# Expert results added back by slot matmuls in SBUF instead of by a trip through DRAM

## The reference

```
x    = layer_norm(ALPHA * x + merged @ w_o)                       # x1, 264 x 2048
combine[t, e]: router; top-1 of 4 expert groups, in it top-2 experts, weights sum to 1
for e in range(16):
    h = silu(xt @ w_gate[e]) * (xt @ w_up[e])                     # 2048 -> 1024
    y = y + combine[:, e:e + 1] * (h @ w_down[e])                 # 1024 -> 2048
x    = layer_norm(ALPHA * x + y)
```

## Time and profile before

| what | us |
|---|---|
| median of three executions | 1874.08 |
| the three | 1872.98, 1874.08, 1878.35 |
| span of the profiled execution | 1878.3 |
| time of the profiled execution | 1878.35 |
| TensorE busy | 1594.0 (85%) |
| VectorE / ScalarE / POOL busy | 623.6 / 363.1 / 95.0 |

### The profile page before, as it was taken

One profiled execution on the slowest core, in us unless ns is written; L12 is line 12 of the kernel. 1 busy time (PEld: TensorE's weight loads), 2 busy tenths in 40 slices (PEclk: granted clock), 3 DMA queues, 4 the chain that ended last, 5 costly groups with the idle time before them and its releaser, 6 DMA issues.

```text
span 1878.3 us, 22982 instructions
## 1 busy us (share of the span) xinstructions
PE 1594.0 (85%) x10115; PEld 1079.2 (57%) x10115; DVE 623.6 (33%) x734; ACT 363.1 (19%) x330; POOL 95.0 (5%) x111
## 2 busy tenths in 40 slices
PE   5999999999999999949987977878879778788760
PEld 5999999988999999934422422324224233242230
DVE  5446687564376565563400100000001000000017
ACT  4454555411244332210000000000000000000011
POOL 3000000011000000020000000000000000000015
PEclk9999999987999999969999999999999999999985
DMA  8855555575546765768999999999999999999953
GB/s 248 267 161 158 156 157 158 157 191 160 155 135 182 250 182 160 254 255 334 415 413 413 415 415 413 413 415 415 414 412 416 415 415 412 416 415 414 411 221 119
DMA packets 311863, 559.98 MB, mean 298 GB/s; under 512 B 6304, under 2 KB 223408, under 8 KB 293976
## 3 DMA queue, kind: packets, MB, share of 16 engines
q1 hardware_dynamic: 304400, 526.60, 76.6%
q0 software_dynamic: 7392, 32.32, 5.1%
HBM read 539.40 MB, written 19.50 MB: 298 GB/s over the span
## 4 chain that ended last, share of the span: by engine, by line
PE 56%; DMA 32%; SPq 5%; DVE 4%; ACT 1%; issue 1%; POOL 0%; POOLq 0%; DVEq 0%; ACTq 0%
DMA ring_low<-wg 12%; PE bank L518 11%; PE bank L519 11%; PE bank L520 11%; DMA ring_high<-wu 9%; DMA ring_low<-wu 8%; PE bank L773 8%; PE bank L754 5%; SPq L343 5%; PE bank L806 3%; DMA ring_low<-w_in 2%; PE bank L561 2%; PE bank L668 1%; PE bank L619 1%; DMA ring_low<-wob 1%
## 5 line engine op out<-in xcount | busy, mean ns | idle before, releaser
L518 PE MATMUL bank<-x_hi,w_hi 128*128 128x264 f32 x1280 | 375.8, 294 | 20.8 <-DVE x_lo L1005 15.8
L519 PE MATMUL bank<-x_lo,w_hi 128*128 128x264 f32 x1280 | 370.9, 290 | 0.0
L520 PE MATMUL bank<-x_hi,w_lo 128*128 128x264 f32 x1280 | 370.4, 289 | 0.0
L996 DVE TENSOR_TENSOR w_lo<-ring_low,w_hi 128x2048 fp32r<-128x2048 f32 x112 | 256.5, 2291 | 158.3 <-ACT w_hi L846 157.4
L773 PE MATMUL bank<-ring_low,reg_pk 128*64 128x512 f32 x1024 | 239.7, 615 | 81.3 <-DMA ring_low<-wg 42.4
L773 PE MATMUL bank<-ring_high,reg_pk 128*64 128x512 f32 x1024 | 229.5, 596 | 47.7 <-DMA ring_high<-wu 40.9
L518 PEld LDWEIGHTS bank<-x_hi,w_hi 128*128 128x128 f32 x1280 | 250.3, 196 | 22.5 <-issue 15.8
L519 PEld LDWEIGHTS bank<-x_lo,w_hi 128*128 128x128 f32 x1280 | 250.2, 195 | 0.1
L520 PEld LDWEIGHTS bank<-x_hi,w_lo 128*128 128x128 f32 x1280 | 248.4, 194 | 0.0
L846 ACT CAST w_hi<-ring_low 128x2048 fp32r<-128x2048 f32 x112 | 212.8, 1900 | 150.4 <-PE bank L520 91.0
L773 PEld LDWEIGHTS bank<-ring_low,reg_pk 128*64 128x64 f32 x1024 | 70.6, 140 | 250.0 <-issue 120.9
(11 more groups left out here) (286 smaller groups left out, 1492.4 us busy)
## 6 DMA issues: line engine op xcount, KB each, us to landing
ring_low<-w_in SPq DMA_DIRECT2D x80, 1024.0 KB, 5.8
ring_high<-wg SPq DMA_DIRECT2D x32, 2048.0 KB, 29.1
ring_low<-wu SPq DMA_DIRECT2D x32, 2048.0 KB, 24.7
ring_high<-wd SPq DMA_DIRECT2D x32, 2048.0 KB, 23.7
ring_low<-wg SPq DMA_DIRECT2D x32, 2048.0 KB, 29.4
ring_high<-wu SPq DMA_DIRECT2D x32, 2048.0 KB, 24.3
ring_low<-wd SPq DMA_DIRECT2D x32, 2048.0 KB, 25.6
ring_low<-wo SPq DMA_DIRECT2D x16, 1024.0 KB, 5.8
```

Of the source, the lines that this page charges most:

```text
L518: pe.matmul(out, hi[k], of_hi[:, k, :], start=(k == 0), stop=False)
L519: pe.matmul(out, hi[k], of_lo[:, k, :], start=False, stop=False)
L520: mm = pe.matmul(out, lo[k], of_hi[:, k, :], start=False, stop=(k == kk - 1))
L996: dve.tensor_tensor(w_lo[:, q % 4, :], raw_w[:, q % 4, :], hi_of(q).bitcast(F32), ALU.subtract).then_inc(lo_ready, 1)
```

## The change

`expert_rows` and everything that touches it goes: the zero fill, the 32 stores, the six indirect loads, the row numbers. In its place there are an accumulator in SBUF, `acc` (two blocks of 128 tokens by 2048) and `acc_s` (the sample tokens, folded so that a quarter of the columns lies on each 32 partitions), which ScalarE fills with ALPHA * x1, and a weighted scatter at the end of each pair: VectorE multiplies `pick` by the router's weights (`weigh`), TensorE transposes it (`pick_transposed`), and then multiplies it by the pair's 128 result rows, one PSUM bank of 512 columns at a time (`scatter`, `N_SC` = 9 banks); VectorE adds each bank to the accumulator (`add_scattered`). Results leave banks 4 and 5 on ScalarE and VectorE, half each. The gather for a ninth pair is made only if there is one. The parameters of the last norm are read by SP behind the last weights, into ring slots. POOL makes a matrix `quarter` and has nothing to do in the end; the last norm is rebuilt over VectorE and ScalarE.

```diff
         def down(i, a, gathered_next=True):
...
+            def pick_transposed(i, first=False):
+                pe.wait_ge(weighted, i + 1)
+                if not first:
+                    pe.wait_ge(sc_ev, i * N_SC)
+                for tt in range(3):
+                    m = P if tt < 2 else 32
+                    mm = pe.transpose(psum[7][:, P * tt:P * tt + m], pick[0:m, tt, :, :].rearrange("p a s -> p (a s)"), ident[0:m, 0:m])
+                mm.then_inc(pick_tr, 1)
+            def scatter(i):
+                pe.wait_ge(ob_act, i * 2 + 3)
+                pe.wait_ge(ob_dve, i * 2 + 3)
+                pe.wait_ge(pick_ev, i + 1)
+                for nn in range(4):
+                    mm = pe.matmul(psum[6][32 * nn:32 * nn + 32, :], pick_t[:, 2 * P:2 * P + 32], ob[:, 512 * nn:512 * nn + 512], start=True, stop=True)
+                mm.then_inc(sc_mm, 1)
+                for b in range(1, N_SC):
+                    tt, nn = divmod(b - 1, 4)
+                    if b > 1:
+                        pe.wait_ge(sc_ev, i * N_SC + (b - 1))
+                    pe.matmul(psum[6 + b % 2][:, :], pick_t[:, P * tt:P * tt + P], ob[:, 512 * nn:512 * nn + 512], start=True, stop=True).then_inc(sc_mm, 1)
-                gather(i + 1)
-                down(i, 1)
+                if not last:
+                    gather(i + 1)
+                down(i, 1, not last)
+                scatter(i)
# ScalarE, in a pair
+                    if a == 0:
+                        act.wait_ge(pick_tr, i + 1)
+                        act.copy(pick_t, psum[7][:, 0:2 * P + 32]).then_inc(pick_ev, 1)
...
+                    act.wait_ge(w_used, i * UNITS + (W_FREE + 12 * a + 12))
+                    act.copy(ob[64 * a:64 * a + 64, 0:512], psum[4][0:64, :])
+                    act.copy(ob[64 * a:64 * a + 64, 512:1024], psum[4][64:128, :]).then_inc(ob_act, 1)
# VectorE, in a pair
+            def add_scattered(i):
+                dve.wait_ge(sc_mm, i * N_SC + 1)
+                dve.tensor_tensor(acc_s, acc_s, psum[6][:, :], ALU.add).then_inc(sc_ev, 1)
+                for b in range(1, N_SC):
+                    tt, nn = divmod(b - 1, 4)
+                    part = acc[:, tt, 512 * nn:512 * nn + 512]
+                    dve.wait_ge(sc_mm, i * N_SC + (b + 1))
+                    dve.tensor_tensor(part, part, psum[6 + b % 2][:, :], ALU.add).then_inc(sc_ev, 1)
# POOL
-            for a in range(2):
-                pool.dma_start(scratch[CAP * (E + 4 * a):CAP * (E + 4 * a + 4), :].rearrange("(p r) c -> p (r c)", p=P),
-                               up[:, 0:4096]).then_inc(zero_out, 16)
...
-            with pool.Fori(0, NPAIR) as i:
-                store_pair(i, i * (2 * CAP))
+            pool.wait_ge(rank_mm, 1)
+            link(pool.memset(quarter, 0.0))
+            for off in range(-3, 4):
+                link(pool.affine_select(out=quarter, in_=quarter, compare_op=ALU.not_equal, fill=0.25, base=32 * off,
+                                        pattern=[[-1, P]], channel_multiplier=1))
# SP, behind the last weights
+            sp.wait_ge(w_used, pairs * UNITS + ((NPAIR - 1) * UNITS + W_FREE + 18))
+            for a, par in enumerate((ln2g, ln2b)):
+                sp.dma_start(ln2p[:, a, :], par.partition_broadcast(P)).then_inc(ln2_in, 16)
+            for a, par in enumerate((ln2g, ln2b)):
+                for nn in range(4):
+                    sp.dma_start(ln2q[32 * nn:32 * nn + 32, a, :], par[512 * nn:512 * nn + 512].partition_broadcast(32)).then_inc(ln2q_in, 16)
# VectorE, the end (ScalarE takes the square roots and the row * 1/std - mean/std)
+            dve.wait_ge(sc_ev, pairs * N_SC + NPAIR * N_SC)
+            link(dve.bn_stats(stat[:, 2, 0, :], acc_s))
...
+            link(dve.tensor_tensor(acc[:, 0, :], acc[:, 0, :], ln2p[:, 0, :], ALU.mult))
...
+            dve.tensor_tensor(acc[:, 0, :], acc[:, 0, :], ln2p[:, 1, :], ALU.add).then_inc(y_ready, 1)
...
+            for cols in (slice(0, D // 2), slice(D // 2, D)):
+                link(dve.tensor_tensor(acc[:, 1, cols], acc[:, 1, cols], ln2p[:, 0, cols], ALU.mult))
+                dve.tensor_tensor(acc[:, 1, cols], acc[:, 1, cols], ln2p[:, 1, cols], ALU.add).then_inc(y_ready, 1)
```

More of the change, by code:

```diff
@@ L69 @@
 LEVELS = 8
+N_SC = 9
 def start_of(name):
@@ L184, in build @@
         before = reg_qg[:, 2 * D:2 * D + P]
+        quarter = before
         small, _ = place("small", [P, 608])
@@ L203, in build @@
         back4 = take(EG)
-        e64 = take(E)
         ecol = take(E)
@@ L239, in build @@
         r1 = t3(2)
-        count, nmore, cum = (rtake(E) for _ in range(3))
+        comb = t3()
+        count, nmore, cum, of_block = (rtake(E) for _ in range(4))
         more, number, which, wtmp = (rtake(4 * E).rearrange("p (e b) -> p e b", b=4) for _ in range(4))
@@ L394, in _ @@
                                     pattern=[[0, 1]], channel_multiplier=-1))
-            for out, base, step, k in ((iota_cap, 0, 1, CAP), (back4, -EG, 1, EG), (e64, 0, CAP, E), (ecol, 0, 1, E), (b64, CAP, CAP, 4)):
+            for out, base, step, k in ((iota_cap, 0, 1, CAP), (back4, -EG, 1, EG), (ecol, 0, 1, E), (b64, CAP, CAP, 4)):
                 link(pool.iota(iota_i[:, 0:k], pattern=[[step, k]], base=base, channel_multiplier=0))
@@ L805, in down, with pair @@
                         for nn in range(4):
-                            mm = pe.matmul(psum[4 + nn // 2][64 * (nn % 2):64 * (nn % 2) + 64, :], hidt[a][:, k % 4, k // 4, :],
+                            mm = pe.matmul(psum[4 + nn // 2][64 * (nn % 2):64 * (nn % 2) + 64, :], hidt[:, k % 4, k // 4, :],
                                            wt[:, kk, 512 * nn:512 * nn + 512], start=(k == 0), stop=(k == 7))
                     mm.then_inc(w_used, 1)
-            def pair(i, gathered=True):
-                expert(i, 0, gathered)
+            def scatter(i):
+                pe.wait_ge(ob_act, i * 2 + 3)
+                pe.wait_ge(ob_dve, i * 2 + 3)
+                pe.wait_ge(pick_ev, i + 1)
+                for nn in range(4):
+                    mm = pe.matmul(psum[6][32 * nn:32 * nn + 32, :], pick_t[:, 2 * P:2 * P + 32], ob[:, 512 * nn:512 * nn + 512], start=True, stop=True)
[5 more added lines that the diff above has]
+                    pe.matmul(psum[6 + b % 2][:, :], pick_t[:, P * tt:P * tt + P], ob[:, 512 * nn:512 * nn + 512], start=True, stop=True).then_inc(sc_mm, 1)
+            def pair(i, first=False, last=False):
+                expert(i, 0, not first)
+                pick_transposed(i, first)
                 down(i, 0)
                 expert(i, 1)
-                gather(i + 1)
-                down(i, 1)
+                if not last:
+                    gather(i + 1)
+                down(i, 1, not last)
+                scatter(i)
             pe.wait_ge(x1s_ready, 1)
             pe.wait_ge(picked, 1)
-            pair(0, gathered=False)
-            with pe.Fori(1, NPAIR) as i:
+            pair(0, first=True)
+            with pe.Fori(1, NPAIR - 1) as i:
                 pair(i)
+            pair(NPAIR - 1, last=True)
             pe.wait_ge(plan_ready, 1)
@@ L824, in _ @@
             with pe.If(pairs > 0):
+                gather(NPAIR)
                 with pe.Fori(0, pairs) as j:
                     pair(j + NPAIR)
-            pe.nop()
+            pe.wait_ge(quarter_ready, 1)
+            for n in range(2):
+                pe.wait_ge(s_part, n + 1)
+                pe.matmul(psum[n][:, 0:1], quarter, mv[:, 2, n:n + 1], start=True, stop=True).then_inc(s_avg, 1)
         @block.scalar
@@ L939, in _ @@
             act.activation(probs, probs, ACT.Exp).then_inc(r_exp, 1)
+            act.wait_ge(x1_ready, 3)
+            act.mul(acc, x1[:, 0:2, :], ALPHA).then_inc(acc_ready, 1)
+            act.wait_ge(x1s_ready, 1)
+            for nn in range(4):
+                ins = act.mul(acc_s[32 * nn:32 * nn + 32, :], x1[0:32, 2, 512 * nn:512 * nn + 512], ALPHA)
+            ins.then_inc(acc_ready, 1)
+            act.sem_inc(ob_act, 1)
             def pair(i):
@@ L1345, in further_block @@
                 link(dve.tensor_tensor(which, which, more, ALU.mult))
+                link(dve.tensor_reduce(of_block, which, AX.X, ALU.add))
                 for tt in range(3):
@@ L1386, in pair, with choose_next @@
+            def choose_next(i):
+                dve.wait_ge(pick_tr, i + 1)
                 choose(i + 1)
+            def pair(i, last=False):
+                weigh(i)
                 hidden(i, 0)
+                if not last:
+                    choose_next(i)
                 result(i, 0)
                 hidden(i, 1)
-                take_gathered(i + 1)
+                if not last:
+                    take_gathered(i + 1)
                 result(i, 1)
-            choose(1)
+                add_scattered(i)
@@ L1405, in _ @@
             result(0, 1)
-            with dve.Fori(1, NPAIR) as i:
+            dve.wait_ge(acc_ready, 2)
+            add_scattered(0)
```

(4 more changed lines are left out.)

192 lines of the change are left out of this document (81 added, 111 removed).

## The result

The changed kernel takes 1822.84 us (median of four executions, 1820.37 to 1824.01), the kernel before 1874.8 beside it (1872.98 to 1878.35): ratio 0.972, 95% interval 0.9706 to 0.9734, 52.0 us less. Timed again in a later set it was 1821.06 beside 1873.87, ratio 0.9718 (0.9697 to 0.9738). The forecast was 1819.5, within 1808 to 1832.

The account below looks back on a forecast made before the run. DMA bounds the pairs; no engine alone sets the last 58 us. 1.7 + 18.2 + 7.0 + 28.6 - 1.0 = 54.5 us off the profiled 1878.3 gives 1823.8, or 1819.5 against the median; range 1808 to 1832.

Parts of the forecast that it names:

- rival A: The forecast itself, each term within its bounds: 1819.5 us, from 1812 to 1826; chance 0.70.
- Step 1: First stage: without the 4 MB zero fill TensorE loses one wait; 1.7 us won, between 0 and 1.7.
- Step 2: Pairs: 30 of 32 stores leave the full DMA path; 17.6 us by spacing, 19.0 by bytes, 18.2 taken.
- Step 3: End of each pair: the scatter holds TensorE 7.7 us, hidden under the weight loads; nothing on the path.
- Step 4: Last pair: without the ninth gather the last `down` next waits for its weights; 7.0 us earlier, not 13.
- Step 5: From the last `down` matmul to the end: the rebuilt tail takes 31.3 us, not 59.9; 28.6 gained.
- Step 6: Before the first gather: POOL's `quarter` selects delay VectorE's normalisation of x1; 1.0 us lost, up to 3.5.
- Rival C: Longer end: additions at 0.94, sample matmuls one by one, or norm parameters delaying last quarters; 1822 to 1831 us; chance 0.14.
- Rival E: Pairs: the scatter's waits drop TensorE's clock to 1.2 GHz, TensorE becomes the bound; 1976 us at a third; chance 0.03.

Follow-up runs that it names:

- the experiment: The changed kernel with the 32 stores of 256 KB put back, to a DRAM table nobody reads: 1839.88 us, 18.8 more than the changed kernel timed again.

## Why the prediction was right, point by point

The time and the mechanism were right: rival A, 1819.5 forecast, 1822.84 measured. The sum was 54.5 us, the medians say 52.0; the 59.8 between the two traces holds some 8 us that are not the change's. A part of the closeness is luck: the stores and the tail were put 3.5 us too high together, the fill and `quarter` 2.7 too low, and these nearly cancel.

- **Step 1, the zero fill, 1.7.** 3.5 by the medians, about 2.3 of waits by the trace. The mechanism was right, and the bound "between 0 and 1.7" too tight: it had only the one wait of 1.68 in it, where the waits for `w_lo` in that stage add up to 5.1 in the same trace.
- **Step 2, the stores, 18.2.** 16.4 to 16.8 by the traces, 18.8 by the medians of the experiment, which hold some of the first stage. The pairs came out at 121.7 where 121.8 was forecast. The price by bytes (19.0) was the wrong half of the mean; the count of 7.5 pairs by the spacing of 2.35 gives 17.6, and 16.6 is seven pairs' worth. That the norm's parameters cost nothing held: issued at 1757.4, they land 25.7 and 29.6 us later and nobody waits.
- **Step 3, the scatter, hidden.** Right that it is hidden, wrong in its size: 10.2 us a pair and not 7.7. What was wrong is "both say about 2 cycles a column at 2.4 GHz". It took the four matmuls of 1.98 us in the earlier trace rows, and the 24 of 2.94, for as many as the trace counts; they are half as many, each twice as long. The gather's 96 records beside 48 matmuls in the code could have shown it beforehand. The Trainium skill (FP8 and Floating Point Precision, TensorE Precision Notes), which the prediction set aside with "The rows decide", says four passes for float32. The estimate of 0.85 us a bank that the prediction worked out from this agrees with the 0.86 measured, and the step of 0.94 with the 0.953 of the additions. The additions end 2.3 us later than forecast, where 2 had been put on it: about 1.9 of them are the wider step and 0.5 the later first bank, for the narrow matmuls took 1.07 and not 0.6. In the pairs the error cost nothing, since there is cover for some 12 us more.
- **Step 4, the last gather, 7.0.** 7.1 in the trace of the changed kernel, 7.2 in the trace and 7.8 by the medians when done alone. What was late next was the weights, as said.
- **Step 5, the tail, 28.6.** 26.7. The additions end at 10.95 and not at 8.6, which is the whole miss, and the rest took 22.25 against 22.7. The part that POOL had held up is 10.4 us by experiment.
- **Step 6, `quarter`, 1.0.** 0.1. The two engines do shut each other out, but here the one that waited was POOL, and nobody waited for it.

The sum by what was measured: 3.5 (medians) + 16.6 + 7.1 + 26.7 - 0.1 = 53.8 us, against 52.0 and 52.8 in two sets; a rest of 1 to 2 us is of the size of the ranges. Rival C's condition, additions at 0.94, did come; 1822.84 lies in its range and in A's, the 1821.06 of the second set only in A's.

Rival E did not come: the granted clock in the pairs is 0.99. Its hint was read rightly, though. In the kernel before the clock was 0.53 from 1141.4 to 1145.0, behind the wait of 2.47, and that makes the 8.78 of the earlier trace rows. In the changed kernel it is 0.51 from 1101.6 to 1105.0, at the start of a `down` that takes 15.65 us, behind two waits of 0.88 and 0.76; behind the same two waits one pair later (1223.39) the `down` takes 13.95, so these waits alone don't decide it. Such a `down` costs 1.7 us of TensorE. The cover of the changed kernel hides it, and only with the scatter three times over does it show in the length of the pair (123.95, not 122.27).

What stays open is what decides between the early executions: why the first gather of kernels with the same first stage starts 5 us apart. They differ in the granted clock of the first 60 us (0.94, 0.97 or 1.00) and in that of 380 to 480 us (0.80 to 0.83), and no run here sets it. Open too is why span and time lie only 0.05 us apart in the profiled run of the kernel before.

## What to carry to other kernels

Where loads fill the DMA engines without a gap, take bytes off the queue first: each 1.05 MB was worth 2.2 to 2.45 us here (123.88 against 121.66 with only the stores put back, 124.15 against 121.70 between the two kernels), while 10 us of new TensorE work a pair cost nothing. Issuing that work two and three times shows how much cover is left. Check a price by counting a row's instructions against the code: a count that doesn't match makes every price "per instruction" wrong by that factor. When a kernel's last engine changes, price the tail by what each engine still does there; two that work at once may be two that take turns, as VectorE and POOL did here.

## What was unexpected of the hardware

- A float32 matmul stands in the trace as two: 8 in the code, x16 in the row, 0.43 us apart, 0.86 us each with 512 columns at full width. A transpose stands as one. A quarter's 8 matmuls with weights of 64 columns take 3.65 us, 0.46 each against the 0.86 at full width, so two of those run beside one another.
- Four matmuls with 32 columns of weights took 1.07 us in all, not four times 0.86, so they too run beside one another.
- VectorE and POOL blocked one another both ways: a VectorE pass of 2.35 us grew to 6.46 beside POOL's of 6.42, and seven selects of POOL grew from 2.90 to 6.18 beside VectorE's passes, which lost 0.03 us each.
- Between the last addition and the first statistics VectorE stands 0.55 us, with nothing else to wait for; between additions, which wait for TensorE, only 0.18 or 0.35.
